# Level 0 of the delta rule's triangular inverse made by VectorE with its 32x32 transpose, and a prologue that loads by ring slot

## What is computed

```python
a = rmsnorm(h, norm_g[l, 0]) * (1.0 + sc1) + sh1        # sh1, sc1 from silu(c) @ w_ada
mix, cb, shg, sgd = token_mixer(a, ...)                 # proj = a @ w_in, HGRN2 branch, delta net branch
h = h + g1 * rmsnorm(mix, norm_g[l, 1])
a = rmsnorm(h, norm_g[l, 2]) * (1.0 + sc2) + sh2
h = h + g2 * rmsnorm(jnp.square(jax.nn.relu(a @ w_up)) @ w_down, norm_g[l, 3])
```

```python
gam = jnp.cumsum(g_, axis=-1)
L = jnp.exp(jnp.where(incl, gam[..., :, None] - gam[..., None, :], -jnp.inf))
kb = k_ * b_[..., None]
A = jnp.where(strict, jnp.einsum('bhtd,bhsd->bhts', kb, k_) * L, 0.0)
X = lax.linalg.triangular_solve(A + eye, rhs, left_side=True, lower=True, unit_diagonal=True)
```

## Time and profile before

| what | value |
|---|---|
| median of 3 launches | 3835.84 us (3831.84 to 3843.88) |
| the profiled execution, its own time | 3828.32 us |
| its span | 3826.8 us |
| TensorE matmul busy | 3615.3 us, 94% |
| VectorE (DVE) busy | 2218.9 us, 58% |
| ScalarE (ACT) busy | 1805.4 us, 47% |
| GpSimd (POOL) busy | 875.6 us, 23% |
| TensorE's granted clock, mean | 0.957 |
| HBM | 587.95 MB by DMA, mean 154 GB/s |

### The profile page before, as it was taken

One profiled execution on the slowest core, in us unless ns is written; L12 is line 12 of the kernel. 1 busy time (PEld: TensorE's weight loads), 2 busy tenths in 40 slices (PEclk: granted clock), 3 DMA queues, 4 the chain that ended last, 5 costly groups with the idle time before them and its releaser, 6 DMA issues.

```text
span 3826.8 us, 78578 instructions
## 1 busy us (share of the span) xinstructions
PE 3615.3 (94%) x25051; PEld 3301.5 (86%) x25051; DVE 2218.9 (58%) x4395; ACT 1805.4 (47%) x3850; POOL 875.6 (23%) x1035
## 2 busy tenths in 40 slices
PE   8899999999899999989999999999895999999997
PEld 2599999998889888888889898897684999999996
DVE  2466666646665666556555656546667545455555
ACT  1345445455544445546445444454463434444443
POOL 1022222201155444440344554411100000000000
PEclk9999999999999999999999999999996999999998
DMA  8645445469633334338543333368882555555553
GB/s 283 191 140 146 141 138 147 138 186 284 194 99 104 96 105 124 96 101 265 160 118 96 105 96 97 101 168 254 249 248 78 162 159 163 159 161 158 163 159 112
DMA packets 887591, 587.95 MB, mean 154 GB/s; under 512 B 23602, under 2 KB 820244, under 8 KB 886932
## 3 DMA queue, kind: packets, MB, share of 16 engines
q1 hardware_dynamic: 861268, 510.50, 46.6%
q0 software_dynamic: 26240, 76.41, 6.5%
HBM read 545.83 MB, written 40.99 MB: 153 GB/s over the span
## 4 chain that ended last, share of the span: by engine, by line
PE 81%; DVE 7%; issue 5%; ACT 3%; DMA 2%; POOL 1%; DVEq 0%; SPq 0%; ACTq 0%; POOLq 0%
PE acc L574 20%; PE acc L576 19%; PE acc L575 19%; PE acc L547 3%; PE bank L784 2%; PE bank L770 2%; PE bank L804 2%; PE bank L819 1%; ACT whi L991 1%; PE bank L586 1%; DVE wlo L1465 1%; PE bank L587 1%; DVE h_S L1619 1%; PE bank L768 1%; PE bank L657 1%
## 5 line engine op out<-in xcount | busy, mean ns | idle before, releaser
L1465 DVE TENSOR_TENSOR wlo<-raw,whi 128x512 fp32r<-128x512 f32 x1799 | 1285.9, 732 | 982.3 <-ACT whi L991 963.5
L991 ACT ACTIVATE whi<-raw 128x512 fp32r<-128x512 f32 x1799 | 1098.7, 628 | 955.2 <-PE acc L576 897.4
L574 PE MATMUL acc<-ahi,whi 128*128 128x288 f32 x4112 | 1311.3, 319 | 41.8 <-DVE alo L1957 16.2
L575 PE MATMUL acc<-alo,whi 128*128 128x288 f32 x4112 | 1239.2, 301 | 0.0
L576 PE MATMUL acc<-ahi,wlo 128*128 128x288 f32 x4112 | 1234.5, 300 | 0.0
L574 PEld LDWEIGHTS acc<-ahi,whi 128*128 128x128 f32 x4112 | 797.5, 194 | 66.0 <-issue 45.5
L575 PEld LDWEIGHTS acc<-alo,whi 128*128 128x128 f32 x4112 | 799.0, 194 | 13.2 <-issue 11.5
L576 PEld LDWEIGHTS acc<-ahi,wlo 128*128 128x128 f32 x4112 | 799.0, 194 | 0.0
L574 PE MATMUL acc<-ohi,whi 128*128 128x288 f32 x1792 | 539.2, 301 | 22.2 <-DVE olo L1993 9.6
L575 PE MATMUL acc<-olo,whi 128*128 128x288 f32 x1792 | 533.7, 298 | 0.0
L576 PE MATMUL acc<-ohi,wlo 128*128 128x288 f32 x1792 | 532.3, 297 | 0.0
(11 more groups left out here) (431 smaller groups left out, 4556.7 us busy)
## 6 DMA issues: line engine op xcount, KB each, us to landing
raw<-in_w_in SPq DMA_DIRECT2D x386, 512.0 KB, 4.1
raw<-in_w_ada SPq DMA_DIRECT2D x192, 512.0 KB, 4.7
raw<-in_w_up SPq DMA_DIRECT2D x128, 512.0 KB, 4.1
raw<-in_w_down SPq DMA_DIRECT2D x128, 512.0 KB, 3.8
raw<-in_w_out_gdn SPq DMA_DIRECT2D x64, 512.0 KB, 5.0
raw<-in_w_o SPq DMA_DIRECT2D x34, 512.0 KB, 5.0
raw<-in_w_out_hg SPq DMA_DIRECT2D x32, 512.0 KB, 5.3
g_S<-in_state_gdn POOLq DMA_DIRECT2D x32, 512.0 KB, 5.9
```

Source lines behind the costliest of these rows:

```text
L574: mm(bank[:, 0:T], whi[:, s, r, :], hi[:, kt, :], start=(kt == 0), stop=False, skip_group_check=True)
L575: mm(bank[:, 0:T], whi[:, s, r, :], lo[:, kt, :], start=False, stop=False, skip_group_check=True)
L991: f(whi[:, s], raw[:, r], ACT.Copy).then_inc(sg["hi_made"], 1)
L1465: tt_(wlo[:, s], raw[:, r], whi[:, s].bitcast(F32), SUB).then_inc(sg["lo_made"], 1)
```

## The change

Level 0 of A is a product of k.k between neighbour tokens 2m+1 and 2m, beta, and one step's decay. Three new columns of `tab` (31 to 33) hold -beta times the exponential of the token's own log decay. VectorE masks k.k with `levm[:, 0]` once for both heads, and a scalar_tensor_tensor multiplies it by that column and adds the identity: that is T. VectorE's 32x32 transpose of T gives U, since level 0 has nothing outside the 32x32 blocks on the diagonal. TensorE's turn, GpSimd's level 0 and its T go. `glevs` now lies in `gPUs`. In the prologue, each of the first four loads of w_in waits for its own ring slots, `alo` is subtracted by GpSimd, the fourth piece's `split_hi` stands ahead of the last four tiles, and the memsets of `tab` and `xs` stand behind `cst`.

```diff
-        tab = sb("tab", [P, GH, 31])
+        tab = sb("tab", [P, GH, 34])
...
                 if isinstance(free, int) and free <= 0:
-                    sp.wait_ge(sg["ada_used"], ADA_PARTS)
+                    sp.wait_ge(sg["ada_used"], ADA_PARTS - RAW // 2 + at.slot(piece, RAW) // 2 + 1)
...
-                if s == 6:
-                    pe.wait_ge(sg["g_lev"], 6 * n + 1)
-                    for p in range(4):
-                        turn(R[2][:, p * P:(p + 1) * P], glev[:, 0, p, :], ident[:, :])
-                    for e in range(2):
-                        last = turn(R[4][0:NS, e * NS:(e + 1) * NS], glevs[:, 0, e, :], ident[0:NS, 0:NS])
-                    last.then_inc(sg["g_l1"], 1)
                 if s in PU:
                     l = PU.index(s) + 1
-                    pe.wait_ge(sg["g_lev"], 6 * n + l + 1)
+                    pe.wait_ge(sg["g_lev"], 5 * n + l)
...
             for k in range(AHEAD):
                 split_hi(pos(S_BG), k - AHEAD)
+            split_hi(pos(S_BG), 0)
             a_out(ADA_BLOCKS // 2 - 1)
-            slab_hi(pos(S_BG), 0)
+            for k in range(1, 4):
+                split_hi(pos(S_BG), k)
...
+                    act.wait_ge(sg["bg_taken"], 1)
+                    f(bge[:, 0:2, :], bgT[:, 0:2, GH:2 * GH], ACT.Exp)
+                    f(bge[0:NS, 2, :], bgT[0:NS, 2, GH:2 * GH], ACT.Exp)
...
-            nc.vector.memset(tab[:, :, :], 0.0)
-            for rows_ in (slice(NS, 2 * NS), slice(2 * NS, P)):
-                nc.vector.memset(xs[rows_, :], 0.0)
             dve.wait_ge(sg["c_exp"], 1)
...
+            nc.vector.memset(tab[:, :, :], 0.0)
+            for rows_ in (slice(NS, 2 * NS), slice(2 * NS, P)):
+                nc.vector.memset(xs[rows_, :], 0.0)
...
-                    dve.wait_ge(sg["a_hi"], max(j - 1, 0))
+                    dve.wait_ge(sg["a_lo"], max(j - 1, 0))
...
-                    dve.wait_ge(sg["a_hi"], j + 1)
-                    tt_(alo[:, j, :], atmp[:, j % 2, :], ahi[:, j, :].bitcast(F32), SUB).then_inc(sg["a_lo"], 1)
...
+                    stt(tab[0:m, :, 31 + a], bgT[0:m, a, 0:GH], -1.0, bge[0:m, a, :], MUL, MUL)
...
                     last.then_inc(sg["g_a"], 1)
+                    dve.wait_ge(sg["g_w"], n)
+                    dve.wait_ge(sg["g_uts"], EARLIER + n)
+                    tt_(gUi[:, 0:2, :], R[6][:, :].rearrange("p (a k s) -> p a k s", a=2, k=2)[:, :, 0, :],
+                        levm[:, 0, :].unsqueeze(1).to_broadcast([P, 2, P]), MUL)
+                    tt_(gUs[0:NS, 0, :], R[5][0:NS, 128:160], levm[0:NS, 0, 0:NS], MUL).then_inc(sg["g_y"], 1)
...
                 if s == 5:
+                    dve.wait_ge(sg["g_y"], EARLIER + n + 1)
+                    dve.wait_ge(sg["g_ut"], 5 * n)
+                    for a in range(2):
+                        for e in range(2):
+                            stt(gT[:, 2 * a + e, :], gUi[:, a, :], gsc[:, e, 31 + a:32 + a], ident[:, :], MUL, ADD)
+                    for e in range(2):
+                        last = stt(gTs[:, e, :], gUs[0:NS, 0, :], gsc[0:NS, e, 33:34], ident[0:NS, 0:NS], MUL, ADD)
+                    last.then_inc(sg["g_t1"], 1)
+                    dve.wait_ge(sg["g_t1"], n + 1)
+                    flip(gUi[:, :, :].rearrange("p q s -> p (q s)"), gT[:, :, :].rearrange("p q s -> p (q s)"))
+                    flip(gUs[0:NS, :, :].rearrange("p e s -> p (e s)"), gTs[:, :, :].rearrange("p e s -> p (e s)")).then_inc(sg["g_u1"], 1)
                     silu_z(2 * n + 2, 1)
-                if s == 7:
-                    dve.wait_ge(sg["g_l1"], EARLIER + n + 1)
-                    tt_(gUi[:, :, :], ident[:, :].unsqueeze(1).to_broadcast([P, 4, P]), R[2][:, :].rearrange("p (q s) -> p q s", s=P), SUB)
-                    tt_(gUs[0:NS, :, :], ident[0:NS, 0:NS].unsqueeze(1).to_broadcast([NS, 2, NS]),
-                        R[4][0:NS, 0:2 * NS].rearrange("p (e s) -> p e s", s=NS), SUB).then_inc(sg["g_u1"], 1)
...
+            for j in range(KT):
+                pool.wait_ge(sg["a_hi"], j + 1)
+                pool.wait_ge(sg["a_tmp"], j + 1)
+                pt(alo[:, j, :], atmp[:, j % 2, :], ahi[:, j, :].bitcast(F32), SUB).then_inc(sg["a_lo"], 1)
...
             def prev(n, between=None, cache=False):
-                level(n, 0)
                 level(n, 1)
-                pool.wait_ge(sg["g_lev"], 6 * n + 1)
-                pool.wait_ge(sg["g_tnew"], 4 * n)
-                pt(gT[:, :, :], ident[:, :].unsqueeze(1).to_broadcast([P, 4, P]), glev[:, 0], SUB)
-                pt(gTs[:, :, :], ident[0:NS, 0:NS].unsqueeze(1).to_broadcast([NS, 2, NS]), glevs[:, 0], SUB).then_inc(sg["g_t1"], 1)
                 level(n, 2)
```

More of the change, by code:

```diff
@@ L55 @@
 COUNTS_ON = {
-    "g_d": "h_turned", "g_kk": "h_ds", "g_l1": "h_ss", "g_uts": "h_o", "g_ss": "h_qexp", "g_ssln": "h_ln",
+    "g_d": "h_turned", "g_kk": "h_ds", "g_y": "h_ss", "g_uts": "h_o", "g_ss": "h_qexp", "g_ssln": "h_ln",
     "g_rs": "h_gexp", "g_qkt": "h_tok", "g_qpt": "h_sq", "g_ex": "h_ssln", "g_wcp": "h_rs", "g_ocp": "h_e",
@@ L239, in hybrid_layer @@
             bgs = sb("bgs", [P, 576])
+            bge = sb("bge", [P, 3, GH])
             with ExitStack() as part:
@@ L297, in hybrid_layer @@
             glev = sb("g_lev", [P, 2, 4, P])
-            glevs = sb("g_levs", [NS, 2, 2, NS])
             gQKm = sb("g_QKm", [P, 2, P])
@@ L308, in hybrid_layer @@
             gPUs = sb("g_PUs", [NS, 2, NS])
+            glevs = gPUs
             gQW = sb("g_QW", [P, 2, NB, 2, TS])
@@ L320, in hybrid_layer @@
             gn2 = sb("g_n2", [P, 2, T])
-            gsc = sb("g_sc", [P, 2, 31])
+            gsc = sb("g_sc", [P, 2, 34])
             gcw = sb("g_cw", [P, 4, 4])
@@ L772, in delta_second @@
                         for e in range(2):
-                            last = mm(R[5][0:NS, e * NS:(e + 1) * NS], glevs[:, 1, e, :], gUs[0:NS, e, :], start=True, stop=True)
+                            last = mm(R[5][0:NS, e * NS:(e + 1) * NS], glevs[:, e, :], gUs[0:NS, e, :], start=True, stop=True)
                     last.then_inc(sg["g_pu"], 1)
@@ L779, in delta_second @@
                         pe.wait_ge(sg["g_t1"], n + 1)
-                        pe.wait_ge(sg["g_qkm"], EARLIER + n + 1)
                     else:
@@ L1376, in _ @@
             ts, tt_, stt, rec = nc.vector.tensor_scalar, nc.vector.tensor_tensor, nc.vector.scalar_tensor_tensor, nc.vector.reciprocal
-            copy = nc.vector.tensor_copy
+            copy, flip = nc.vector.tensor_copy, nc.vector.transpose
             MUL, ADD, SUB = ALU.mult, ALU.add, ALU.subtract
@@ L1502, in _ @@
             slab_lo(pos(S_BG), 0)
+            dve.wait_ge(sg["a_lo"], KT)
             for rows_ in (slice(NS, 2 * NS), slice(2 * NS, P)):
@@ L1767, in delta_prev @@
                     dve.wait_ge(sg["g_kk"], EARLIER + n + 1)
-                    dve.wait_ge(sg["g_lev"], 6 * n)
+                    dve.wait_ge(sg["g_lev"], 5 * n)
                     dve.wait_ge(sg["g_attn"], n)
@@ L1794, in delta_prev @@
                     dve.wait_ge(sg["g_u1"], EARLIER + n + 1)
-                    dve.wait_ge(sg["g_t1"], n + 1)
                     dve.wait_ge(sg["g_unew"], 5 * n + l - 1)
@@ L2228, in level @@
             def level(n, l):
-                if l == 0:
+                if l == 1:
                     pool.wait_ge(sg["g_a"], EARLIER + n + 1)
                     pool.wait_ge(sg["g_pu"], 5 * n)
-                if l == 2:
-                    pool.wait_ge(sg["g_l1"], EARLIER + n + 1)
-                    pool.wait_ge(sg["g_t1"], n + 1)
                 if l > 2:
@@ L2237, in level @@
                 last = pt(glev[:, l % 2], gA[:, :, :], levm[:, l, :].unsqueeze(1).to_broadcast([P, 4, P]), MUL)
-                if l < 2:
-                    last = pt(glevs[:, l], gAs[:, :, :], levm[0:NS, l, 0:NS].unsqueeze(1).to_broadcast([NS, 2, NS]), MUL)
+                if l == 1:
+                    last = pt(glevs[:, :, :], gAs[:, :, :], levm[0:NS, 1, 0:NS].unsqueeze(1).to_broadcast([NS, 2, NS]), MUL)
                 last.then_inc(sg["g_lev"], 1)
             def prev(n, between=None, cache=False):
-                level(n, 0)
                 level(n, 1)
-                pool.wait_ge(sg["g_lev"], 6 * n + 1)
-                pool.wait_ge(sg["g_tnew"], 4 * n)
-                pt(gT[:, :, :], ident[:, :].unsqueeze(1).to_broadcast([P, 4, P]), glev[:, 0], SUB)
-                pt(gTs[:, :, :], ident[0:NS, 0:NS].unsqueeze(1).to_broadcast([NS, 2, NS]), glevs[:, 0], SUB).then_inc(sg["g_t1"], 1)
                 level(n, 2)
```

## The result

The change makes the kernel slower: 3864.95 us (median of 5 runs, 3857.76 to 3875.21) against 3835.84 us for the kernel before, measured beside it. The ratio is 1.0075, with a 95% interval of 1.0055 to 1.0094. The forecast was 3803 us with a range up to 3852, so the result lies outside, 1 us from the rival called "shut out" (3866).

What follows compares the result with a forecast made beforehand. TensorE, busy 94% of the span, was taken as the bound. Passes 23.1 us (48.2 saved less 25.1 new wait), clock 4 and prologue 6 sum to 33 us; forecast 3803 us against 3835.8, range 3791 to 3852.

Steps and rivals of the forecast that it cites:

- shut out: Rival, delta passes: a VectorE instruction behind the split is held while GpSimd runs on; wait 4.8 us, 3866 us, chance 0.16.
- VectorE's part: Delta passes: VectorE's masks, split, decays and transposes run uninterrupted; new TensorE wait 1.57 us a pass, 25.1 us in all.
- The turns that go: TensorE in the delta passes: removing its level 0 turns saves 0.81 us a pass, 13.0 us over 16.
- old waits: TensorE's waits at the turn (31.1 us, for GpSimd) and at L770 (4.1 us, for VectorE) would go.
- The clock: Delta passes: a shorter TensorE stop should bring fewer half-clock stretches; 4 us gained, bounds nothing to 14 us.
- The prologue: Before the passes: earlier w_in loads, first split and last quarter, and memsets moved behind cst; together 6 us gained.
- the 1 us for the earlier start: Prologue: memsets moved behind cst free up to 1.76 us each, but w_ada loads must arrive; 1 us taken.
- The last quarter: Prologue, last quarter of the first slab: should start at 142 to 143 instead of 147.81; 5 us, between 3 and 6.
- the alternation: Rival, delta passes: every decay lets one GpSimd instruction through; TensorE waits 3.6 us a pass, 3843 us, chance 0.28.

Runs made afterwards that it cites:

- pool_held: The changed kernel, with GpSimd waiting for VectorE's transposes before level 2; 3800.75 us, ratio to before 0.991.
- decay_bank: The changed kernel, its large decays reading k.k from its bank and multiplying by the identity (computes another inverse; only times count); 3823.98 us, ratio 0.9974.
- prologue_only: The kernel before, with only the four prologue edits of the change; 3831.48 us, ratio to before 0.9994.
- first_held: The changed kernel with mask and decays ahead of A, transposes behind the mask of q.k, and GpSimd waiting for g_z before level 2; 3802.37 us.

## Why the prediction was wrong

**The step that failed** is the one in VectorE's part that let the four decays go 0.26 us apart, "as the four of L1772", to end at 5.0. Those of L1772 read one SBUF tensor and a bank, the decays two SBUF tensors. In every pass one decay took 3.0 us. All before it was right to 0.1 us: A ended at 1.66 (1.63), the split was issued at 2.51 (2.5) and ran until 3.66 (3.65), TensorE stood at L764 at 4.61 (4.63). All behind it was right as well: the transposes took 0.71 and 0.19 us (0.67 and 0.2). The 1.24 us that the prediction worked out from the Trainium skill's 311 ns (VectorE: DVE Perf Modes, The three transpose paths), a figure for bf16, doesn't hold for these float32 blocks. The decays, small ones included, ended at 7.76 in place of 5.0, so the wait was 4.16 us a pass and 66.7 in all, where I had 1.57 and 25.1: a wait mis-sized by 41.6 us. With the 19 us of the clock and the 2 to 4 of the prologue, below, that is the 62 us between forecast and result, give or take 3.

**The turns that go** were put at 13.0 us for 16 passes, 12.2 for the 15 of the stage. The rest of the stage, without idle time and clock, became 14.6 us shorter with the change and 10.5 in the mean of the eleven kernels without turns, so the term was about right. The 35.2 us of old waits went as forecast.

**The clock** had the wrong sign: 4 us to be gained, 15.2 lost in the stage. It went with the same step, as a stop of 4.2 us instead of 1.98 came with more half clock; in pool_held, with a stop of 1.46 us, the clock gave 8.8 us back. That the longer stop brings it is argued from such pairs, and decay_bank, below, doesn't fit.

**The prologue** was put at 6 us and gave 2 by the ratio of prologue_only, 4 by the mean end of k.k. The term that failed is the 1 us for the earlier start: the parts of w_ada didn't come sooner, and TensorE lost the start again to their wait and, in four kernels, to half clock; the modulation ended at 133.0 in the mean of the ten, at 131.8 and 132.6 in the two without. The last quarter was forecast at 142 to 143; it came at 145.75 in the change, at 142.09 in first_held, and at 143.3 in the mean of the ten, against 147.81 and 148.38.

**The rivals.** The right one was described with its rows: g_z's 3.34 us in pass 0, and the same in pass 14. It got 0.16, "but these are two of 16, and there the instruction behind the split was another one". Counting was the wrong way to weigh it; the trace of before says what sets the two passes apart. In passes 1 to 13 the split starts 0.26 us behind GpSimd's mask (1219.46 and 1219.72 in the earlier trace rows), runs its 0.67 us, and it is the mask that is held (2.43 us). In pass 0 it starts 0.35 us behind it:

```profile
1054.41 1.28 POOL L2237 TENSOR_TENSOR g_lev<-g_A,levm 128x512 f32<-128x512 f32 x1 [2.77 <-DVE g_As L1774]
...
1054.76 1.48 DVE L1465 TENSOR_TENSOR wlo<-raw,whi 128x512 fp32r<-128x512 f32 x1
```

There the mask has its 1.28 us, the split is held, and so is g_z behind it; pass 14 is the same. In pass 15 g_z starts 0.35 us behind the mask and goes first, so 0.35 lies on the edge:

```profile
2449.90 2.51 POOL L2237 TENSOR_TENSOR g_lev<-g_A,levm 128x512 f32<-128x512 f32 x1 [7.78 <-DVE g_As L1774]
...
2450.25 0.43 DVE L1763 TENSOR_TENSOR g_z<-g_ca,g_ce 128x288 f32<-128x288 f32 x1
```

The change puts the new mask of k.k between A and the split, which I had priced at 0.43 us and carried into the split's time: 2.5 instead of 2.06. That makes the distance 0.69 to 0.77 us in passes 0 to 14, well past the edge, and GpSimd goes first in all of them. The prediction had that much: its split waits for level 1 and runs until 3.65. It then sent the decays through the rest of GpSimd's row as if VectorE were ahead again. The rival's price came within 1 us of the result, and that was luck, as its parts were off: 4.8 us of wait where 4.16 came, 8 us for the clock where the stage lost 15.2, and 6 for the prologue where 2 to 4 came. Of the alternation, in which every decay lets one GpSimd instruction through, no pass showed anything.

**What stays open.** Why a held instruction gets through at the end of level 1 but not at the end of level 2. The start times don't tell: in pass 2 the held decay stands at 1223.91, 0.22 us ahead of level 2 (1224.13) and 0.53 behind the small level, and it still waits for level 2 and both masks. That the distance of 0.3 us decides was read from these passes and not tried by itself. And what sets the number of half-clock stretches: they don't follow the stop alone, as decay_bank has stops of 3.2 us a pass and the least half clock of all, 92.3 us. (It also multiplies other numbers; whether that bears on the clock was not tried.)
